# Two stacked blocks, the first microseconds: half of the input is loaded before any weights, and the first projection's products are put in another order

## The reference, cut to what matters

```python
def first_block(x, g_mix, w_in, ...):
    h = rms_norm(x, g_mix)      # per token: x * rsqrt(mean(x*x) + eps) * g_mix
    z = h @ w_in                # (512, 1024) @ (1024, 3072)
    u, gb, gc, q, k, v = split(z)
    ...                         # short convolution, three-branch attention, w_out, gated FFN
```

## Time and profile before

| | |
|---|---|
| time, median of 3 runs | 978.46 us (977.72 to 980.54) |
| the profiled execution | 977.04 us |
| its span, first to last instruction | 975.5 us |
| mean granted TensorE clock | 0.997 |
| PE busy | 963.5 us, 99% of the span |
| DVE, ACT, POOL busy | 685.3, 413.4, 187.2 us |

### The profile page before, as it was taken

One profiled execution on the slowest core, in us unless ns is written; L12 is line 12 of the kernel. 1 busy time (PEld: TensorE's weight loads), 2 busy tenths in 40 slices (PEclk: granted clock), 3 DMA queues, 4 the chain that ended last, 5 costly groups with the idle time before them and its releaser, 6 DMA issues.

```text
span 975.5 us, 13907 instructions
## 1 busy us (share of the span) xinstructions
PE 963.5 (99%) x4623; PEld 777.0 (80%) x4623; DVE 685.3 (70%) x1226; ACT 413.4 (42%) x684; POOL 187.2 (19%) x321
## 2 busy tenths in 40 slices
PE   8999999999999999999999999999999999999996
PEld 7777777787888888888888886888888887677886
DVE  5886785798766665755346568489889876785756
ACT  5564353644323332323221226945652325663234
POOL 3010111120100000187200001745670220100000
PEclk9999999999999999999999999999999999999998
DMA  7346757332653333334423223333233462653222
GB/s 231 110 95 193 208 166 191 84 90 86 178 174 101 104 90 90 104 108 129 142 97 95 99 77 103 93 87 87 61 91 89 120 161 83 148 152 122 86 88 108
DMA packets 143766, 115.13 MB, mean 118 GB/s; under 512 B 5516, under 2 KB 131724, under 8 KB 143724
## 3 DMA queue, kind: packets, MB, share of 16 engines
q1 hardware_dynamic: 135468, 85.88, 29.9%
q0 software_dynamic: 8240, 28.73, 10.9%
q10 hardware_dynamic: 16, 0.00, 0.0%
HBM read 100.44 MB, written 4.20 MB: 107 GB/s over the span
## 4 chain that ended last, share of the span: by engine, by line
PE 96%; DVE 1%; ACT 1%; DMA 1%; issue 0%; SPq 0%; DVEq 0%; ACTq 0%
PE bank L655 19%; PE bank L657 19%; PE bank L656 19%; PE bank L940 4%; PE bank L938 4%; PE bank L939 4%; PE bank L638 2%; PE bank L639 2%; PE bank L640 2%; PE bank L689 2%; PE bank L709 2%; PE bank L827 1%; PE bank L829 1%; PE bank L828 1%; PE bank L1155 1%; PE bank L1154 1%
## 5 line engine op out<-in xcount | busy, mean ns | idle before, releaser
L655 PE MATMUL bank<-hH,wH 128*128 128x512 f32 x792 | 310.8, 392 | 0.8 <-DVE gt L1990 0.8
L657 PE MATMUL bank<-hH,wL 128*128 128x512 f32 x792 | 308.5, 390 | 0.0
L656 PE MATMUL bank<-hL,wH 128*128 128x512 f32 x792 | 308.5, 389 | 0.0
L1682 DVE TENSOR_TENSOR wL<-raw,wH 128x1024 fp32r<-128x1024 f32 x155 | 195.4, 1261 | 139.0 <-ACT wH L1198 138.7
L1198 ACT ACTIVATE wH<-raw 128x1024 fp32r<-128x1024 f32 x155 | 164.1, 1059 | 287.1 <-PE bank L657 126.9
L655 PEld LDWEIGHTS bank<-hH,wH 128*128 128x128 f32 x792 | 148.7, 188 | 38.8 <-issue 7.9
L657 PEld LDWEIGHTS bank<-hH,wL 128*128 128x128 f32 x792 | 148.7, 188 | 31.1
L656 PEld LDWEIGHTS bank<-hL,wH 128*128 128x128 f32 x792 | 148.8, 188 | 30.1
L938 PE MATMUL bank<-aH,wH 128*128 (+1 forms) x160 | 62.3, 389 | 0.0
L939 PE MATMUL bank<-aL,wH 128*128 (+1 forms) x160 | 62.3, 389 | 0.0
L940 PE MATMUL bank<-aH,wL 128*128 (+1 forms) x160 | 62.3, 389 | 0.0
(11 more groups left out here) (494 smaller groups left out, 1570.0 us busy)
## 6 DMA issues: line engine op xcount, KB each, us to landing
raw<-in_w_in_dram SPq DMA_DIRECT2D x61, 512.0 KB, 3.6
mraw<-in_w_mod_dram POOLq DMA_DIRECT2D x24, 512.0 KB, 5.0
raw<-in_w_gate_dram SPq DMA_DIRECT2D x22, 512.0 KB, 3.7
raw<-in_w_up_dram SPq DMA_DIRECT2D x22, 512.0 KB, 3.7
raw<-in_w_down_dram SPq DMA_DIRECT2D x22, 512.0 KB, 3.2
raw<-in_w_out_dram SPq DMA_DIRECT2D x16, 512.0 KB, 3.5
pTd<-turned POOLq DMA_DIRECT2D x24, 320.0 KB, 6.7
x_tok<-in_x_dram SPq DMA_DIRECT2D x8, 256.0 KB, 6.2
```

What stands on the lines that cost most here:

```text
L655: mm(o, a, hH[:, k, :], start=(k == 0), stop=False)
L656: mm(o, a, hL[:, k, :], start=False, stop=False)
L657: ins = mm(o, b, hH[:, k, :], start=False, stop=(k == KD - 1))
L1682: TT(wL[s.par][:], raw[s.par][:], wH[s.par][:].bitcast(F32), SU).then_inc(lo_done, 1)
```

## The change

SP issues the four first-half pieces of the input first, then the query slot in two halves of four feature blocks each (256 KB, in two DMAs with a semaphore each), then the second-half pieces. ACT and DVE no longer split the first slot as a whole before the input: they split it in two halves between their steps on `hH` and `hL`. ACT does `x_copy(0)` behind `hH` 1, and `x_copy` of 3 and 2 behind `hH` 3 and the second half, ahead of `hH` 4. PE transposes the identity four times more, turns the whole second half (with `k` = 7) of token blocks 0 and 1 between the products of `k` = 0 and `k` = 1, and of token blocks 2 and 3 ahead of `k` = 2. It makes wH·hH and wH·hL for `k` 0 to 3 and only then the four wL·hH; for `k` 4 to 7 the three products stand together as before. The counts of `h1h` and `h1_done` include the halves' signals. `glu_full` is now `w_part`, with one more signal of 16 ahead of those it had.

```diff
+        def h1h_count(k):
+            return 1 if k == 0 else k + 2
+        def h1_count(k):
+            return k + 1 if k < 2 else k + 2
...
-            load(Slot(N_MIX), cols(w_in, Z_Q))
-            for h in range(2):
+            def x_half(h):
+                c = slice(h * HALF, h * HALF + HALF)
                 for t in range(TB):
-                    c = slice(h * HALF, h * HALF + HALF)
                     sp_.dma_start(x_tok[:, t, c], x[0, t * P:(t + 1) * P, c]).then_inc(x_in[t][h], 16)
+            def query_half(h, done):
+                c = slice(h * KH, h * KH + KH)
+                sp_.dma_start(raw[0][:].rearrange("p (k c) -> p k c", k=KD)[:, c, :], cols(w_in, Z_Q)[:, c, :]).then_inc(done, 16)
+            x_half(0)
+            query_half(0, w_part)
+            query_half(1, w_full[0])
+            x_half(1)
             load(Slot(N_MIX, 1), cols(w_in, Z_K))
...
             for t in range(TB):
                 x_turn(t, range(KH))
                 transposes(PB[6], [ident] * 2)
+            transposes(PB[6], [ident] * 4)
             transposes(PB[6], [ident] * 2)
-            x_turn(0, range(KH, KD - 1))
-            x_turn(1, range(KH, KD - 1))
...
             def project_first():
+                def product(w, h, k):
+                    return mm(PB[7][:], blk(w[0], k), h[:, k, :], start=(k == 0 and w is wH and h is hH), skip_group_check=True,
+                              stop=(k == KD - 1 and w is wL))
+                pe.wait_ge(vec_cp, 1)
+                for k in range(KH):
+                    pe.wait_ge(h1h, 2 if k == 0 else h1h_count(k))
+                    product(wH, hH, k)
+                    pe.wait_ge(h1_done, h1_count(k))
+                    product(wH, hL, k)
+                    if k == 0:
+                        pe.wait_ge(xt_a, 1)
+                    if k < 2:
+                        x_turn(2 * k, range(KH, KD))
+                        x_turn(2 * k + 1, range(KH, KD))
+                for k in range(KH):
+                    product(wL, hH, k)
                 pe.wait_ge(lo_done, 1)
-                pe.wait_ge(vec_cp, 1)
-                for k in range(KD):
-                    if k == 2:
-                        x_turn(2, range(KH, KD - 1))
-                        x_turn(3, range(KH, KD - 1))
-                    if k == KH:
-                        pe.wait_ge(xt_a, 1)
-                        for t in range(TB):
-                            x_turn(t, [KD - 1])
-                    pe.wait_ge(h1_done, k + 1)
-                    mm(PB[7][:], blk(wH[0], k), hH[:, k, :], ...)
-                    mm(PB[7][:], blk(wH[0], k), hL[:, k, :], ...)
-                    ins = mm(PB[7][:], blk(wL[0], k), hH[:, k, :], ...)
+                for k in range(KH, KD):
+                    pe.wait_ge(h1_done, h1_count(k))
+                    product(wH, hH, k)
+                    product(wH, hL, k)
+                    ins = product(wL, hH, k)
                 ins.then_inc(slot_used, 1)
...
+            def query_high(h):
+                c = slice(h * HALF, h * HALF + HALF)
+                act.wait_ge((w_part, w_full[0])[h], 16)
+                copy(wH[0][:, c], raw[0][:, c]).then_inc((h1h, hi_done)[h], 1)
...
-            split_hi(Slot(0))
             act.wait_ge(vec_cp, 1)
             for k in range(KD):
                 act.wait_ge(xn_mm, k + 1)
                 A(hH[:, k, :], HB[k][:], ACT.Identity, scale=...).then_inc(h1h, 1)
+                if k == 0:
+                    query_high(0)
+                if k == 1:
+                    x_copy(0)
                 if k == KH - 1:
-                    x_copy(0)
+                    query_high(1)
+                    x_copy(3)
+                    x_copy(2)
             split_hi(Slot(1))
...
             split_hi(Slot(2))
-            for k in (3, 2, 7):
-                x_copy(k)
+            x_copy(7)
...
-            split_lo(Slot(0))
+            def query_low(h):
+                c = slice(h * HALF, h * HALF + HALF)
+                dve.wait_ge((h1h, hi_done)[h], 2 - h)
+                TT(wL[0][:, c], raw[0][:, c], wH[0][:, c].bitcast(F32), SU).then_inc((h1_done, lo_done)[h], 1)
+
             dve.wait_ge(vec_cp, 1)
             for k in range(KD):
-                dve.wait_ge(h1h, k + 1)
+                dve.wait_ge(h1h, h1h_count(k))
                 STT(hL[:, k, :], ...).then_inc(h1_done, 1)
-            x_copy(1)
+                if k == 1:
+                    query_low(0)
+                if k == KH - 1:
+                    query_low(1)
+                    x_copy(1)
```

More of the change, by code:

```diff
@@ L269, in program @@
         x_in = [[sem(f"x_in{t}{h}") for h in range(2)] for t in range(TB)]
-        cst_in, mask_in, glu_full, vec_in, vecp_in, svec_in, s5_in, out_done = (
-            sem(n) for n in ("cst_in", "mask_in", "glu_full", "vec_in", "vecp_in", "svec_in", "s5_in", "out_done"))
+        cst_in, mask_in, w_part, vec_in, vecp_in, svec_in, s5_in, out_done = (
+            sem(n) for n in ("cst_in", "mask_in", "w_part", "vec_in", "vecp_in", "svec_in", "s5_in", "out_done"))
         w_full = [sem(f"w_full{s}") for s in range(2)]
@@ L431, in at_ @@
                     src = w_glu_2[0].rearrange("(k p) c -> p k c", p=P)[:, :, bass.ds(i * P + e * HALF, P)]
-                    sp_.dma_start(dst, src).then_inc(glu_full if e else w_full[s.par], 16)
+                    sp_.dma_start(dst, src).then_inc(w_part if e else w_full[s.par], 16)
                 if not last:
@@ L840, in project_first @@
             def project_first():
-                pe.wait_ge(lo_done, 1)
-                pe.wait_ge(vec_cp, 1)
-                for k in range(KD):
-                    if k == 2:
-                        x_turn(2, range(KH, KD - 1))
-                        x_turn(3, range(KH, KD - 1))
-                    if k == KH:
-                        pe.wait_ge(xt_a, 1)
-                        for t in range(TB):
-                            x_turn(t, [KD - 1])
-                    pe.wait_ge(h1_done, k + 1)
-                    mm(PB[7][:], blk(wH[0], k), hH[:, k, :], start=(k == 0), stop=False, skip_group_check=True)
-                    mm(PB[7][:], blk(wH[0], k), hL[:, k, :], start=False, stop=False, skip_group_check=True)
-                    ins = mm(PB[7][:], blk(wL[0], k), hH[:, k, :], start=False, stop=(k == KD - 1), skip_group_check=True)
+                def product(w, h, k):
[14 more added lines that the diff above has]
+                    product(wL, hH, k)
+                pe.wait_ge(lo_done, 1)
+                for k in range(KH, KD):
[3 more added lines that the diff above has]
+                    ins = product(wL, hH, k)
                 ins.then_inc(slot_used, 1)
@@ L1225, in x_copy @@
             def x_copy(k):
-                act.wait_ge(h1_done, k + 1)
+                act.wait_ge(h1_done, h1_count(k))
                 copy(xT[:, k, :], HB[k][:]).then_inc(xt_a, 1)
+            def query_high(h):
+                c = slice(h * HALF, h * HALF + HALF)
+                act.wait_ge((w_part, w_full[0])[h], 16)
+                copy(wH[0][:, c], raw[0][:, c]).then_inc((h1h, hi_done)[h], 1)
             act.wait_ge(cst_in, 16)
             copy(identP[:].rearrange("k (p j) -> k p j", j=TB), ident.rearrange("k (j p) -> k p j", j=TB))
-            split_hi(Slot(0))
             act.wait_ge(vec_cp, 1)
@@ L1554, in _ @@
             gate(s, tga[:, KD - 1, :])
-            act.wait_ge(glu_full, 16)
+            act.wait_ge(w_part, 32)
             split_hi(s.next())
@@ L1571, in att @@
                 if not last:
-                    act.wait_ge(glu_full, i * 16 + 32)
+                    act.wait_ge(w_part, i * 16 + 48)
                 split_hi(s.next())
```

## The result

| | before | changed |
|---|---|---|
| median of 22 runs each, in turn | 977.75 us | 979.26 us |
| lowest and highest | 977.10 to 980.54 | 977.25 to 984.89 |
| the profiled execution | 977.04 us | 983.26 us |
| its span | 975.5 us | 981.7 us |

The ratio is 1.0017, with an interval of 1.001 to 1.0024: the changed kernel is 1.0 to 2.3 us slower. That is within the 0.3% bound, and the forecast of +1.0 is its lower edge. The changed kernel also goes above 980 us more often: in 8 of its 22 executions, where the kernel before does so in 1 of 22. Its profiled execution is one of the longest, 6.2 us above that of before. It shows everything at its largest, so I read it first and then ask how typical it is.

What follows compares the result with a forecast made beforehand. PE, busy 99% of the span, was taken to bound the kernel; 0.67 us won ahead was given back, with more, in PE's waits, so the first projection ends 1.0 later: 978.46 + 1.0 = 979.5 us, range 977.3 to 981.1.

Steps and rivals of the forecast that it cites:

- Loads: Input at the start: fourth piece lands at about 7.6 us instead of 9.4, the query's halves by 9.4.
- First turns: PE's first transposes: two waits go, so the fourth turn starts at 8.71 us instead of 9.38, a gain of 0.67.
- ACT, DVE and the added wait: First projection: two copies delay hH 4 some 1.2 us, PE waits 0.8 for hL 4, end 19.27 against 18.25.
- Does it last to the end: Behind the first projection: engines follow PE, so +1.0 us stays; later small loads, with ldt, covered by 0.7 and 0.8.
- The clock: PE after its 0.8 us stall: clock expected to stay up, so +1.0 us stays; a fall was not excluded.
- third rival: Clock falls in the stall for hL 4, the twelve products behind take 2.8 us more: +3.8, 982.3 us; chance 0.04.
- 0.76 us row: Profile row of a PE wait of 0.76 us after which the clock stayed up, cited for the stall being harmless.
- a rule by which every wait of PE sets the clock back: Trainium skill's rule: PE waiting between groups of products starts the next cold; the sum would be the third rival's.
- Rival 1: First projection: the stall for hL 4 doesn't come, PE ends at 18.46, +0.2 us, 978.7; chance 0.15.
- rival 4: Input no faster than before, fourth piece at 9.4, so the 0.67 is not won: +1.7 us, 980.2; chance 0.14.
- Rival 2: First projection: PE never waits once begun and ends at 17.82, a gain of 0.4 us, 978.0; chance 0.05.

Runs made afterwards that it cites:

- e1: Changed kernel with the three loads behind svec_in (two 8 KB rows and ldt) issued ahead of the value slot; ratio 0.9991 to the kernel before.
- e2: Changed kernel with the copies of blocks 3 and 2 put back behind the value slot's split; ratio 1.0009 to the kernel before.
- e5: Changed kernel with POOL's two 512 KB w_mod loads held until the three loads behind svec_in have landed; ratio 0.9997 to the kernel before.
- e8: The changed kernel measured once more with no edit; ratio 1.0011 to the kernel before.
- e4: Kernel before with the value slot's load and the eleven small loads behind it waiting for hL of block 4; ratio 1.0039.
- e6: Kernel before with three idle DVE products ahead of diag, so that PE waits about 3.3 us; ratio 1.0058.
- e3: Changed kernel with the edits of e1 and e2 together, three loads first and two copies back; ratio 0.9991 to the kernel before.
- e7: Kernel before with a new load order alone: first-half input pieces, the first slot as one load, then the second half; ratio 1.0008.
- e9: Changed kernel with the edits of e1, e2 and e5 joined; ratio 0.9993 to the kernel before.
- e10: e9 without the two identity transposes behind each of the four turns; ratio 0.9991 to the kernel before.

## Why the prediction came out right, point by point

The forecast was +1.0 us (979.5) and the measured ratio says +1.0 to +2.3; the median was 979.26. The number is right, but its parts are not. The forecast median came so near because two errors met: its base, 978.46 from three runs, lay 0.7 us above the 977.75 of twenty-two, and the difference between the medians, 1.5 us, is larger than the 1.0 forecast.

- **Loads.** Right. The fourth piece landed at 7.4 (forecast 7.6), the halves of the slot at 8.2 and 9.0 (by 9.4), the second halves in their places.
- **First turns.** The start of the fourth turn, 8.71, was mis-sized as a fixed number. It took the moment of the full clock from the one profile at hand. Measured: 7.80 to 9.27 with this load order. Where the full clock came as in that profile (7.5 us), the sum was close: e1, with 7.6, had the turn at 8.87 and the end of the projection at 19.21, against 8.71 and 19.27. The word that PE reaches the fourth piece late by itself was right; that this makes PE's start depend on its clock, which the input's landing had hidden, was missed.
- **ACT, DVE and the added wait.** Right in mechanism and close in size. From the fourth turn to the end of the projection the sum gave 19.27 − 8.71 = 10.56 us; four profiles have 10.3. `hH` 4 started straight behind the two copies (15.07); the gap for `hL` 4 was 0.5 us (forecast 0.8), and e2 removed it by putting the copies back. But this was the whole of the forecast +1.0, and the times don't show it: with the late loads out of the way and all of it left in, e1 and e5 allow at most +0.2 and +0.5 us.
- **Does it last to the end.** This step failed. It had the right objects: eleven loads issued 2 us later behind the second half's low part, POOL's transfers beside them, DVE's copies of `ldt`, `diag`, PE. But it let `ldt` land at most one microsecond beyond its old 2.8 and called the rest covered. It took 4.8 to 6.8 us in the profiles of the changed kernel, e8 and e2, and PE waited 1.3 to 2.6 us; e4 shows that the late loads alone make the kernel before 1.9 to 5.8 us slower. The cover was counted in DVE's and PE's time (0.7 and 0.8 us), the landing's own spread was not.
- **The clock.** The third rival had the wrong place: the stall for `hL` 4 (0.5 us) never made the clock fall, the wait for `diag` did, in both profiles of the changed kernel. Its price of 2.8 us was twice what these two show, 1.4 and 1.5; e6's was 2.6 to 2.9. The 0.76 us row was no warrant for 1.5 us and more. Nor do the runs bear out a rule by which every wait of PE sets the clock back: it fell with waits of 1.51, 2.57 and 3.25 us and not with 1.33, 1.43 and 1.75.
- **Rival 1** (no stall for `hL` 4) is out, the gap was there; **rival 4** (input no faster) is out, the piece landed at 7.4. **Rival 2** (a gain) gave 17.82 for the end of the projection; the changed kernel's best by its 10.3 us is 18.1, for a turn at 7.80 as e3 had it. e3 itself ended at 17.61, but with the copies moved as well.

So the +1.0 in the first projection is worked out as −0.2 to +1.3 by execution against the 18.25 of one profile, and in the times it is at most +0.2 (e1) to +0.5 us (e5). The late loads, which the prediction priced at nothing, bring most of the measured loss, if not all of it. That this comes near the forecast +1.0 is luck. The width of the range (to 981.1) held the median, while single executions went to 984.9 through the part that was called covered.

## What to carry to other kernels

When a load moves behind a new wait, list everything queued behind it on the issuing engine, and ask for each what other transfers it will now share the engines with: here 128 bytes took 6.8 us in a profile in which a weight slot of 512 KB takes 3.7 in the median. Count a landing's cover against the longest time such a load could take under that traffic, not against the time it took when the queues were quiet. And when a wait at the start is removed, look for what it was hiding: here a start-up time of PE that differs by microseconds from one execution to the next.

## What the runs showed of the hardware that I had not expected

- PE's first record of the full clock stands between 5.2 and 8.4 us in eleven profiles here and at 10.2 in e6's, although PE begins at 2.27 us in each. Until then four transposes take up to 1.12 us instead of 0.60.
- A wait of PE makes the clock fall only sometimes, and not by its length alone: it stayed up behind 1.33, 1.43 and 1.75 us; it fell with 1.51 us (1.5 us more until the sums of squares), 2.57 (1.4 more) and 3.25 (2.6 to 2.9 more).
- A 128-byte load took 2.8 us just ahead of two 512 KB loads of another queue (before, e6, e7), 3.5 with them held back (e5), and 4.2 to 6.8 us just behind them. Issued at 13 to 14 us, before all of this, it took 1.6 to 1.8 (e1, e3, e9, e10).
